# Plain down projection in the last third of each feed-forward block, and squares that start before a small load lands

## What is computed

```python
def rmsnorm(x, g):
    y = xf * lax.rsqrt(jnp.mean(xf * xf, axis=-1, keepdims=True) + EPS)
    return (y * g)
def swiglu(x, wg, wu, wd):
    return (jax.nn.silu(x @ wg) * (x @ wu)) @ wd
# for each layer:
x = x + 0.5 * swiglu(rmsnorm(x, norm_g[layer, 0]), ffn_w_gate[layer, 0], ffn_w_up[layer, 0], ffn_w_down[layer, 0])
x = x + mix(rmsnorm(x, norm_g[layer, 1]))
x = x + 0.5 * swiglu(rmsnorm(x, norm_g[layer, 2]), ffn_w_gate[layer, 1], ffn_w_up[layer, 1], ffn_w_down[layer, 1])
```

## Time and profile before

| | us |
|---|---|
| median of 3 runs (lowest, highest) | 1884.78 (1884.55, 1885.92) |
| the profiled execution | 1884.31 |
| its span, first to last instruction | 1882.5 |
| TensorE busy in it | 1854.4 (99%) |
| VectorE busy | 1357.2 (72%) |
| ScalarE busy | 820.4 (44%) |
| GpSimd busy | 370.1 (20%) |

### The profile page before, as it was taken

One profiled execution on the slowest core, in us unless ns is written; L12 is line 12 of the kernel. 1 busy time (PEld: TensorE's weight loads), 2 busy tenths in 40 slices (PEclk: granted clock), 3 DMA queues, 4 the chain that ended last, 5 costly groups with the idle time before them and its releaser, 6 DMA issues.

```text
span 1882.5 us, 26452 instructions
## 1 busy us (share of the span) xinstructions
PE 1854.4 (99%) x10116; PEld 1581.4 (84%) x10116; DVE 1357.2 (72%) x2018; ACT 820.4 (44%) x1344; POOL 370.1 (20%) x271
## 2 busy tenths in 40 slices
PE   8999999999999999999999999999999999999998
PEld 6898988878688988988889898888777788989888
DVE  6686866976466867768868586796766666768677
ACT  5343343543243433434534343455565543433433
POOL 0210402412300303114121040242111002104022
PEclk9999999999999999999999999999999999999999
DMA  4244232132032222322323223212222222322322
GB/s 176 81 140 118 90 113 89 69 134 92 22 121 97 97 102 87 113 100 80 112 73 129 90 90 112 90 68 94 75 84 73 72 101 91 107 110 90 113 90 68
DMA packets 65914, 181.34 MB, mean 96 GB/s; under 512 B 13608, under 2 KB 26569, under 8 KB 65802
## 3 DMA queue, kind: packets, MB, share of 16 engines
q1 hardware_dynamic: 52192, 169.89, 26.1%
q10 hardware_dynamic: 13610, 9.93, 1.9%
HBM read 177.70 MB, written 3.93 MB: 96 GB/s over the span
## 4 chain that ended last, share of the span: by engine, by line
PE 90%; DVE 6%; issue 2%; ACT 1%; DMA 1%; SPq 0%; ACTq 0%; DVEq 0%
PE bank L1262 23%; PE bank L1264 23%; PE bank L1263 23%; PE bank L1214 6%; PE bank L1217 5%; PE bank L1218 5%; DVE wlr L446 2%; DVE x L954 1%; PE bank L1374 1%; PE bank L1541 1%; PE bank L1525 1%; PE bank L1387 1%; PE bank L1365 1%; DVE xl L833 1%; ACT xh L549 1%
## 5 line engine op out<-in xcount | busy, mean ns | idle before, releaser
L1262 PE MATMUL bank<-xh,whr 128*128 128x512 f32 x1408 | 551.1, 391 | 3.1 <-DVE xl L833 1.9
L1263 PE MATMUL bank<-xl,whr 128*128 128x512 f32 x1408 | 548.4, 389 | 0.0
L1264 PE MATMUL bank<-xh,wlr 128*128 128x512 f32 x1408 | 548.1, 389 | 0.0
L437 ACT ACTIVATE whr<-rest 128x512 fp32r<-128x512 f32 (+1 forms) x445 | 271.8, 616 | 448.7 <-PE bank L1264 443.0
L446 DVE TENSOR_TENSOR wlr<-rest,whr 128x512 fp32r<-128x512 f32 (+1 forms) x445 | 350.1, 791 | 114.4 <-ACT whr L437 112.0
L1262 PE MATMUL bank<-hsh,whr 128*128 128x256 f32 x1232 | 351.6, 285 | 14.5 <-DVE x L954 7.1
L1263 PE MATMUL bank<-hsl,whr 128*128 128x256 f32 x1232 | 348.5, 283 | 0.0
L1264 PE MATMUL bank<-hsh,wlr 128*128 128x256 f32 x1232 | 348.4, 283 | 0.0
L1262 PEld LDWEIGHTS bank<-xh,whr 128*128 128x128 f32 x1408 | 264.6, 188 | 61.5 <-issue 2.8
L1263 PEld LDWEIGHTS bank<-xl,whr 128*128 128x128 f32 x1408 | 264.7, 188 | 55.5 <-issue 1.2
L1264 PEld LDWEIGHTS bank<-xh,wlr 128*128 128x128 f32 x1408 | 264.6, 188 | 55.2
(11 more groups left out here) (184 smaller groups left out, 2262.4 us busy)
## 6 DMA issues: line engine op xcount, KB each, us to landing
rest<-in_ffn_w_up SPq DMA_DIRECT2D x62, 512.0 KB, 4.7
rest<-in_ffn_w_gate SPq DMA_DIRECT2D x61, 512.0 KB, 3.8
rest<-in_ffn_w_down SPq DMA_DIRECT2D x42, 512.0 KB, 4.3
raw_area<-in_ffn_w_gate SPq DMA_DIRECT2D x26, 512.0 KB, 3.8
raw_area<-in_ffn_w_up SPq DMA_DIRECT2D x26, 512.0 KB, 4.6
raw_area<-in_w_qkv SPq DMA_DIRECT2D x24, 512.0 KB, 3.4
raw_area<-in_ffn_w_down SPq DMA_DIRECT2D x22, 512.0 KB, 4.5
raw_area<-in_w_in_ab SPq DMA_DIRECT2D x16, 512.0 KB, 3.5
```

What stands on the lines that cost most here:

```text
L437: act.activation(whr[:, at:at + st.kb, :].rearrange("p k c -> p (k c)"), weights(st, buf)[:, 0, :], ACT.Copy).then_inc(high, 1)
L1262: pe.matmul(out, whr[:, at, :], hi, start=start, stop=False, skip_group_check=onto)
L1263: pe.matmul(out, whr[:, at, :], lo, start=False, stop=False, skip_group_check=onto)
L1264: return pe.matmul(out, wlr[:, at, :], hi, start=False, stop=stop, skip_group_check=onto)
```

## The change

1. In part three of each feed-forward block the `Down` steps become `Plain` steps: four blocks of 12 passes on 512 columns, no sums of weights or hidden tiles, and two additions of 512 columns into `x` for each pair instead of six.
2. The addition of squares in part three moves from POOL to DVE.
3. The first loads of the phase after a run wait for fewer blocks (8 and 4 instead of 14 and 7), which is again the last two steps and the last one.
4. At the opening ACT no longer waits for the small constants before the squares, but before `norm_std`.

```diff
+class Plain:
+    kind, nblocks, evacs = "plain", 4, 2
...
+        self.bank = (4, 5) if pair % 2 == 0 else (6, 7)
...
-                self.steps += [Down(f, part, pair) for pair in range(KD // 2)]
+                self.steps += [(Down if part < STRASSEN_PARTS else Plain)(f, part, pair) for pair in range(KD // 2)]
...
-                        sp.wait_ge(low, ph.unit0 - (14 if j < 3 else 7) + LOW_CREDIT)
+                        sp.wait_ge(low, ph.unit0 - (8 if j < 3 else 4) + LOW_CREDIT)
...
+                    if st.plain:
+                        act.wait_ge(evac, ph.evac(st, 2) + EVAC_CREDIT)
+                        act.activation(hsh[:, st.k, 0:2, :], he[:, 0:2, :], ACT.Copy).then_inc(hh_done, 1)
+                        return
...
                             if late and n == 0:
+                                act.wait_ge(const_in, 16)
                                 norm_std(0)
...
-                            if n == 5 and st.ends:
+                            if n == 2 and st.kind == "plain":
                                 residual_of(st, 0)
...
             block_high(act, phases[0], 3)
-            act.wait_ge(const_in, 16)
             square(0)
             square(1)
...
+                    if st.kind == "plain":
+                        if n % 2:
+                            d = st.d[n // 2]
+                            add(st, n, x[:, d, :], bank[st.bank[n // 2]][:, :], 1)
+                        return
...
+                        if n < 2 and prev and prev.kind == "plain" and FFN_NEXT[prev.ffn] is not None:
+                            (add_squares_of if n else part_low)(FFN_NEXT[prev.ffn], prev.d[1])
...
+                            if n > 1 and st.kind == "plain" and FFN_NEXT[st.ffn] is not None:
+                                (part_low if n == 2 else add_squares_of)(FFN_NEXT[st.ffn], st.d[0])
+                            results(st, n)
...
+                def plain_block(st, n):
+                    for k in range(st.half):
+                        if st.pair == 0 and n < 2 and k in (0, st.half - 1):
+                            pe.wait_ge(hl_done, st.split0 + 2 * st.half - (0 if n and k else 1))
+                        place = slice(2 * (n % 2), 2 * (n % 2) + 2)
+                        last = group(bank[st.bank[n // 2]][:, :], st.block0 + n, k,
+                                     hsh[:, k, place, :].rearrange("p s t -> p (s t)"),
+                                     hsl[:, k, place, :].rearrange("p s t -> p (s t)"),
+                                     start=n % 2 == 0 and k == 0, stop=n % 2 == 1 and k == st.half - 1)
                     last.then_inc(unit_done, 1)
...
-                    if st.ends and FFN_NEXT[st.ffn] is not None:
-                        for d in st.d:
-                            add_squares(FFN_NEXT[st.ffn], d)
```

More of the change, by code:

```diff
@@ L99, in __init__, with splits_before, sums_before @@
         self.buf, self.sums, self.place, self.into, self.fresh, self.reads = buf, sums, place, into, fresh, reads
+STRASSEN_PARTS = 2
+PAIRS_OF = [sum(half for _, half in PARTS[:part]) for part in range(len(PARTS) + 1)]
+def splits_before(ffn, part, k):
+    of = lambda pairs: 3 * min(pairs, PAIRS_OF[STRASSEN_PARTS]) + 2 * max(0, pairs - PAIRS_OF[STRASSEN_PARTS])
+    return ffn * of(PAIRS_OF[-1]) + of(PAIRS_OF[part] + k)
+def sums_before(ffn, part, k):
+    return 3 * (ffn * PAIRS_OF[STRASSEN_PARTS] + PAIRS_OF[part] + k)
 H_B11, H_T1, H_B21, H_B22, H_T3, H_T2, H_T4 = range(7)
@@ L119, in __init__ @@
         self.tiles = KF * ffn + first + n
-        self.pair = KF // 2 * ffn + first // 2 + n // 2
+        self.split0, self.sum0 = splits_before(ffn, part, n // 2), sums_before(ffn, part, n // 2)
+        self.plain = part >= STRASSEN_PARTS
 class Down:
@@ L132, in __init__ @@
         self.d = (2 * pair, 2 * pair + 1)
-        self.sums0 = SUMS * (KD // 2 * (len(PARTS) * ffn + part) + pair)
-        self.hpair = KF // 2 * ffn + self.first // 2
-        self.ends = part == len(PARTS) - 1
+        self.sums0 = SUMS * (KD // 2 * (STRASSEN_PARTS * ffn + part) + pair)
+        self.split0 = splits_before(ffn, part, 0)
         self.bank = ({"Y": 4, "Z": 5, "X": 6, "W": 7} if pair % 2 == 0 else {"Y": 0, "Z": 1, "X": 2, "W": 3})
+class Plain:
+    kind, nblocks, evacs = "plain", 4, 2
+    def __init__(self, ffn, part, pair):
+        self.ffn, self.part, self.pair = ffn, part, pair
+        self.first, self.half = PARTS[part]
+        self.kb = self.half
+        self.d = (2 * pair, 2 * pair + 1)
+        self.bank = (4, 5) if pair % 2 == 0 else (6, 7)
+        self.split0 = splits_before(ffn, part, 0)
 class Run:
@@ L422, in block_high @@
             st, n = run.blocks[v]
-            if st.kind == "up" or PRODUCTS[n].sums is None:
-                half = n // 2 if st.kind == "up" else int(PRODUCTS[n].buf == B_A22)
+            if st.kind != "down" or PRODUCTS[n].sums is None:
+                half = n // 2 if st.kind != "down" else int(PRODUCTS[n].buf == B_A22)
                 if run.before is None and v == 0:
@@ L435, in block_high @@
             at = v % 4 * (KD // 2)
[L436 removed]
+            buf = B_A11 + n if st.kind != "down" else PRODUCTS[n].buf
             act.activation(whr[:, at:at + st.kb, :].rearrange("p k c -> p (k c)"), weights(st, buf)[:, 0, :],
@@ L576, in ffn_run @@
                             split_high(act, ph.next, 0, 0)
-                        if n == 0 and prev and prev.kind == "down" and prev.ends:
+                        if n == 0 and prev and prev.kind == "plain":
                             residual_of(prev, 1)
@@ L585, in ffn_run @@
                                     even_high(prev)
-                            if n == 0 and prev and prev.kind == "down" and not prev.ends:
+                            if n == 0 and prev and prev.kind == "down":
                                 act.wait_ge(unit_done, ph.unit(st, 0) + UNIT_CREDIT)
@@ L900, in ffn_run, with add_squares_of @@
                 NB = ph.units
+                def add_squares_of(norm, d):
+                    add_squares(norm, d, d % 2)
                 def done(st, n):
@@ L989, in ffn_run @@
                             split_low(dve, ph.next, 0, 0)
-                        if n == 0 and prev and prev.kind == "down" and prev.ends and FFN_NEXT[prev.ffn] is not None:
-                            part_low(FFN_NEXT[prev.ffn], prev.d[1])
+                        if n < 2 and prev and prev.kind == "plain" and FFN_NEXT[prev.ffn] is not None:
+                            (add_squares_of if n else part_low)(FFN_NEXT[prev.ffn], prev.d[1])
                         if st.kind == "up":
@@ L1042, in ffn_run @@
                     split_low(dve, ph.next, 0, 1)
+                    add_squares_of(FFN_NEXT[last.ffn], last.d[1])
             opening = {1: (2, 3), 2: (4, 5), 3: (6, 7)}
@@ L1286, in down_block @@
                         pe.wait_ge(evac, ph.evac(st, pr.reads) + EVAC_CREDIT)
-                    pairs = 3 * (st.hpair + st.half)
+                    pairs = st.split0 + 3 * st.half
                     for k in range(st.half):
@@ L1307, in ffn_run @@
                         pe.wait_ge(low, ph.unit(st, n) + 1 + LOW_CREDIT)
-                        if st.kind == "up":
-                            up_block(st, n)
-                        else:
-                            down_block(st, n)
+                        {"up": up_block, "down": down_block, "plain": plain_block}[st.kind](st, n)
             def norm_mean(norm):
```

45 lines of the change are left out of this document (17 added, 28 removed).

## The result

The changed kernel takes 1870.98 us (median of 4 runs, 1869.97 to 1872.69) against 1884.66 (4 runs, 1884.14 to 1885.92): a ratio of 0.993 with a 95% interval of 0.9918 to 0.9942, 13.7 us less. The profiled execution took 1871.8 us, its span 1870.0 (before 1884.31 and 1882.5).

A forecast was written before the change was run, and what follows sets the result against it. The prediction took the kernel to be bound by TensorE's pace of passes, with DVE stalling it in part three. It summed -10.65 + 1.45 - 0.94 - 4.06 = -14.2 us to 1870.6 us, range 1868.8 to 1875.5.

The forecast's parts named there:

- stages of part three, blocks one to three: Plain steps in part three: 43.54 us each without stalls, gaining 3.60, 3.45 and 3.60 us, together 10.65.
- block four: Part three of block four: little stall to lose, so from 42.28 to 43.73 us, 1.45 us dearer.
- seams, both mixers: Mixers behind blocks one and three: the second unit's 0.47 us loss goes at both places, -0.94 us.
- opening: Start of the kernel: earlier squares, mean's pass at 22.85, third `Up` step at 33.5 instead of 37.56, -4.06 us.
- The passes: Plain steps: 192 passes of 0.2268 us replace 336 of 0.120, 43.54 against 40.31 us, 3.23 us dearer a part.
- The stalls: Part three: 6.8, 6.7 and 6.8 us in blocks one to three, from a full DVE; none expected in plain steps.
- its signs: At the opening: right if the mean's pass starts within 0.5 us of 22.85; wrong if third `Up` step before 32.9 or after 34.3.
- stalls in the plain steps: Rival: stalls of 1 to 4 us a block stay in three blocks, 1873.6 to 1882.6 us; chance 0.08.
- dearer passes: Rival: 512-column passes on the hidden tiles take 0.235 instead of 0.2268 us, 1876.7 us in all; chance 0.03.
- the slower case: Rival in part three: the chain `x`, `xh`, `xl`, squares causes the stalls and stays, 1891.9 us; chance 0.03.
- an opening that gives 0 to 3 us: Rival at the kernel's start: the opening gains only 0 to 3 us, 1871.7 to 1874.7 us; chance 0.10.

The follow-up runs named there:

- e6: Kernel before, with POOL's weight sums of part three cut to 8 of 512 columns; 1864.95 us, ratio 0.9901.
- e7: Kernel before, seven products kept, with only the additions of squares in part three moved from POOL to DVE; 1876.68 us, ratio 0.9963.
- e9: Kernel before, with `xl` of part three written for 64 of 512 columns, POOL unchanged; 1881.32 us, ratio 0.9986.
- e11: The changed kernel unaltered, measured again; 1871.52 us, ratio 0.9927.
- e1: Kernel before, with the opening's edit alone (squares no longer wait for the small constants); 1881.8 us, ratio 0.9986.
- e8: Changed kernel, with the additions of squares put back on POOL; 1871.09 us, ratio 0.9933.
- e2: Changed kernel, with the wait for the small constants put back ahead of the squares; 1874.2 us, ratio 0.9949.
- e5: Changed kernel, with the root's table load ahead of the mean and seven short products kept in part three of block four; 1868.49 us, ratio 0.9917.
- e12: The same kernel as e5, measured a second time; 1868.83 us, ratio 0.9912.
- e3: Changed kernel, with the wait for the small constants moved from the root to the last square, so the table load precedes the mean; 1869.65 us, ratio 0.9924.
- e10: Kernel before, with POOL adding 8 of 512 columns of each tile of squares except the last; 1874.3 us, ratio 0.9945.

## Why the prediction was right

Forecast 1870.6, measured 1870.98, and by its steps (profiled executions, us):

| step | predicted | measured |
|---|---|---|
| stages of part three, blocks one to three | -3.60, -3.45, -3.60 | -3.61, -3.47, -3.62 |
| block four | +1.45 | +1.44 |
| seams, both mixers | -0.94 | -0.42, -0.32 |
| opening | -4.06 | -3.82 at the third `Up` step |
| clock behind the attention's wait | not foreseen | +1.4 |

**The passes.** 192 x 0.2268 = 43.54 was forecast, and 43.52 to 43.53 came, with nothing idle. The price of a pass was taken from the `Up` steps of the same trace and carried over exactly. By the rule of the Trainium skill (TensorE: Matmul & The Clock Gate, Back-to-back issue gap) that the prediction quotes, the 192 long passes would be 4.75 us dearer than undisturbed short ones, an estimate; they were 43.52 - 40.31 = 3.21 us dearer, so here the trace decides. The page gives that rule for a single matmul on its own, which the prediction doesn't say.

**The stalls.** Their cause was named as DVE full because POOL stretched it, and the runs confirm it: 6.2 of the 6.8 us go when the weight sums are cut (e6). The prediction didn't see how sharp the effect is. "Stretched" is a wait for POOL's instruction in hand to end. The prediction counted 7.1 us a step of DVE's work against 9.4, as if the length of the list mattered most; e7 lengthens the list and gains 2.7 us a stage, e9 shortens it and gains 1.35. How the worth of the plain steps divides between their missing sums of weights and their shorter list, no run shows; e6 and e9 suggest that the sums are the larger part.

**The opening.** The mean's pass came at 23.03 (22.85 was forecast), the table load behind it as forecast, the third step at 33.74 (33.5), the idle time before it 0.9 us, as forecast. The same kernel profiled again (e11) had the mean's pass at 23.79 and the third step at 34.41, outside the bounds that the prediction sets as its signs (within 0.5 us of 22.85, before 34.3), so the close agreement of one profile is in part luck. 0.4 of the 3.82 us is an earlier first pass (6.60, before 6.99), which the change didn't make. Over all profiles the stretch of the first `Up` steps took 83.63 to 84.97 us in the six profiles with the wait and 80.83 to 82.13 in the four without it that load the table behind the mean (after, e1, e8, e11): about 3 us on average, so the term was some 1 us too large. The reason shows in the six. Four of them, the kernel before among them, were idle for 3.1 us before the mean, had a granted clock of 0.57 to 0.65 from 26 to 30 us, and took 11.3 to 11.5 us from the mean's pass to the third step. The other two (e2, e7) were idle for 2.0 and 2.15 us, kept the clock at 1.00 and took 9.8 us. So the forecast was read from an execution of the dearer kind, and some 1.6 us of its 4.06 are a fall of the clock that an execution of the old opening need not have.

**The seams.** The second unit lost its stall (5.44 and 0.68 us), but the whole stages up to the next one gave 0.42 and 0.32, not 0.47 each: some of the gain was waited away later.

**The sum.** The measured terms, -10.70 + 1.44 - 0.74 - 3.86 + 1.41, the opening taken up to the end of part one (122.37 before, 118.51 now), give -12.45, the spans differ by 12.5. The forecast of -14.2 for the profiled execution missed by 1.7, of which 1.4 is the clock. That the median came within 0.4 us is in part luck. In the medians the opening alone gave 2.85 us (e1) where 4.06 were forecast, and the rest of the change 10.45 (e2) where 10.14 were; the two misses have opposite signs. The median of a kernel also moves from one set of runs to the next: 1884.14 to 1884.68 for the kernel before, 1870.98 and 1871.52 for the changed one.

Of the rivals, three fell: no stalls in the plain steps, no dearer passes (0.2267 us), and the slower case needed the chain `x`, `xh`, `xl`, squares to be the cause, which stayed in e6 and stalled almost nothing. The fourth, an opening that gives 0 to 3 us, was given a chance of 0.10 and is where the medians came out, at its upper end.

## What to carry to other kernels

Where a DVE instruction seems to vary in length, look what GpSimd has in hand: if the ends keep a fixed distance, it is held, and the cheapest cure here was to move GpSimd's two-operand work away (e7, 2.7 of 3.6 us a stage), before anything is said of the algorithm. Work left on GpSimd does no harm where it falls into a wait of DVE's (e8) or beside an instruction of DVE's that reads PSUM. Saving passes pays only where the engine that must feed them has room: seven products beat eight in block four (e5, e12), and lose by 0.9 us in part three of the other blocks even with the squares moved. In part two they take 40.31 us without a stall, and eight would take 43.5 by the pace of the passes; that was not run. And when a wait is moved from one instruction to a later one, see what stands behind the new place: a table load that ran for nothing may now be on the path (here 0.9 us).

## What was not expected of the hardware

**The clock falls behind the same wait in some executions and not in others.** TensorE stands idle for 1.96 to 1.98 us for ACT's `pt` before the first products of attention with its values, in every kernel here. In 8 of the 13 profiles (after, e2, e5, e7, e8, e9, e11, e12) the granted clock right behind it falls to the lower of the two levels (1.2 of 2.4 GHz; 0.51 to 0.66 on average over the next 3.4 us), and the stage takes 56.7 to 56.9 us; in the other five (before, e1, e3, e6, e10) it stays at 1.00 and the stage takes 55.3. Both groups hold kernels with and without the change. So a drop costs 1.4 to 1.6 us of a profiled execution. How much of the spread between runs of one kernel it makes isn't shown, since the mean clock of a run without a profile doesn't tell where it fell (e3's profiled run has 0.999 without this drop). What decides it is open.

**A held instruction's length says nothing of its size.** An `xl` of 64 columns took up to 1.38 us beside POOL (e9), as long as a held split of 512 columns, and 0.28 us alone. What tells its size is the time from the release to its end: 0.08 us for it, 0.55 for 512 columns.

**The hold is mutual.** POOL's instructions were lengthened by DVE as DVE's were by POOL, from 1.29 to up to 1.75 us, and the longer hold then fell back on DVE's next split.
